# Loading the down weights of the experts from ScalarE's queue in place of SyncE's, in a two-block transformer on one core

## What is computed

```python
def expert_block(args):
    xe, e = args
    return (jax.nn.silu(xe @ w_gate[e]) * (xe @ w_up[e])) @ w_down[e]
```

## Time and profile before

| | us |
|---|---|
| median of 3 executions | 2813.23 |
| lowest and highest of them | 2811.11, 2819.49 |
| the profiled execution's own time | 2816.55 |
| its span (first to last instruction) | 2814.5 |
| PE busy | 2575.6 (92%) |
| DVE busy | 1076.7 (38%) |
| ACT busy | 749.4 (27%) |
| POOL busy | 237.4 (8%) |
| DMA moved | 623.91 MB, mean 222 GB/s |

### The profile page before, as it was taken

One profiled execution on the slowest core, in us unless ns is written; L12 is line 12 of the kernel. 1 busy time (PEld: TensorE's weight loads), 2 busy tenths in 40 slices (PEclk: granted clock), 3 DMA queues, 4 the chain that ended last, 5 costly groups with the idle time before them and its releaser, 6 DMA issues. The chain is left out here.

```text
span 2814.5 us, 51444 instructions
## 1 busy us (share of the span) xinstructions
PE 2575.6 (92%) x20439; PEld 1525.9 (54%) x20439; DVE 1076.7 (38%) x2661; ACT 749.4 (27%) x1601; POOL 237.4 (8%) x405
## 2 busy tenths in 40 slices
PE   7999999999999999999997878789999899888787
PEld 4544655544654467645655555544576466555554
DVE  2582653582653245557221111153443642111114
ACT  1211531211642157521111111143675111111111
POOL 4000011000010000011010001020000111110011
PEclk9999999999999999999999999999999999999999
DMA  9211842222843100236999999973002499999996
GB/s 337 90 60 68 299 144 94 88 75 75 299 128 128 60 1 2 84 149 224 396 389 399 394 405 402 399 280 112 1 2 91 176 346 399 397 403 411 414 403 241
DMA packets 134846, 623.91 MB, mean 222 GB/s; under 512 B 14480, under 2 KB 18672, under 8 KB 106496
## 3 DMA queue, kind: packets, MB, share of 16 engines
q1 hardware_dynamic: 103424, 519.68, 47.6%
q0 software_dynamic: 31232, 101.57, 10.5%
HBM read 573.59 MB, written 47.61 MB: 221 GB/s over the span
## 5 line engine op out<-in xcount | busy, mean ns | idle before, releaser
L1236 PE MATMUL PJ<-WR,XT 128*128 128x512 f32 (+2 forms) x1152 | 475.3, 568 | 5.7 <-ACT XT L182 2.8
L182 ACT ACTIVATE PT<-TR 128x512 f32<-128x512 f32 (+3 forms) x384 | 172.9, 480 | 962.2 <-PE TR L1468 832.7
L1236 PEld LDWEIGHTS PJ<-WR,XT 128*128 128x128 f32 x1152 | 215.6, 191 | 243.9 <-issue 215.7
L182 DVE TENSOR_TENSOR PR<-G 128x256 f32<-128x256 f32 (+1 forms) x64 | 29.6, 463 | 686.6 <-ACT G L182 686.2
L1445 PE MATMUL SC<-QK,XT 128*64 128x256 f32 x2112 | 244.3, 385 | 39.1 <-DMA QK<-in_w_up_dram 25.4
L1445 PE MATMUL SC<-WR,XT 128*64 128x256 f32 x1984 | 228.6, 383 | 43.1 <-DMA WR<-in_w_up_dram 25.3
L1194 PE MATMUL PJ<-WR,XT 128*128 128x512 f32 x576 | 254.4, 597 | 3.4 <-ACT XT L182 2.5
L182 DVE TENSOR_REDUCE SM<-SC 128x1 f32<-128x768 f32 (+6 forms) x208 | 173.7, 835 | 172.1 <-PE SC L1214 167.2
L1396 PE MATMUL PJ<-WR,XT 128*128 128x512 f32 x512 | 227.4, 596 | 1.0 <-issue 1.0
L1445 PEld LDWEIGHTS SC<-QK,XT 128*64 128x64 f32 x2112 | 154.6, 138 | 123.6 <-DMA QK<-in_w_up_dram 35.4
L1445 PEld LDWEIGHTS SC<-WR,XT 128*64 128x64 f32 x1984 | 141.5, 138 | 126.9 <-DMA WR<-in_w_up_dram 35.3
(11 more groups left out here) (277 smaller groups left out, 2766.7 us busy)
## 6 DMA issues: line engine op xcount, KB each, us to landing
QK<-in_w_gate_dram SPq DMA_DIRECT2D x34, 2048.0 KB, 23.7
WR<-in_w_down_dram SPq DMA_DIRECT2D x34, 2048.0 KB, 20.2
QK<-in_w_up_dram SPq DMA_DIRECT2D x32, 2048.0 KB
WR<-in_w_up_dram SPq DMA_DIRECT2D x32, 2048.0 KB
WR<-in_w_gate_dram SPq DMA_DIRECT2D x30, 2048.0 KB, 23.4
QK<-in_w_down_dram SPq DMA_DIRECT2D x30, 2048.0 KB
WR<-in_w_ada_dram SPq DMA_DIRECT2D x24, 2048.0 KB, 8.8
WR<-in_w_in_dram SPq DMA_DIRECT2D x14, 2048.0 KB, 7.8
```

The lines of the kernel that those rows point to most:

```text
L182: return lambda *a, **k: Signal(make(*a, **k), self)
L1236: m = mm(bank[:, 0:n], XT1[:, c, s.t * P:(s.t + 1) * P], w[:, c, 0:n], start=c == 0, stop=c == DC - 1)
```

## The change

`load_expert` moves out of SP's function and gets the issuing engine as an argument. SP loads d0 and d1 as before, and from then on only gate and up weights. ACT waits once for the table `ORD`, and loads d2 before its step of place 1; at the end of each of its steps r it waits until `down(r)` is done, reads the expert's number of place r+2 from `ORD`, and issues d(r+2) on its own queue. Its last loads are d30 and d31; its step 30 is written out without a load. Buffers, semaphores, shapes and the order on PE stay.

```diff
--- before.py
+++ after.py
@@ -1053,6 +1053,19 @@
             for r in range(evenly.stop, end):
                 go(lambda a, b: b, r)
 
+        def load_expert(eng, u, e, near_rows=False):
+            tile = slot_tile(u.slot)
+            name = {"gate": "w_gate_2", "up": "w_up_2", "down": "w_down_2"}[u.kind]
+            src = ins[name][u.l, bass.ds(e, 1), :, :].rearrange("e k n -> (e k) n")
+            if u.kind == "down" and near_rows:
+                eng.dma_start(tile.rearrange("p (h x) -> p h x", h=2), src.rearrange("(h p c) n -> p h (c n)", h=2, c=2)).then_inc(
+                    w_loaded[u.slot], 16)
+            elif u.kind == "down":
+                eng.dma_start(tile.rearrange("p (c n) -> p c n", c=4), src.rearrange("(c p) n -> p c n", p=P)).then_inc(
+                    w_loaded[u.slot], 16)
+            else:
+                eng.dma_start(tile, src.rearrange("(p c) n -> p (c n)", p=P)).then_inc(w_loaded[u.slot], 16)
+
         block = ctx.enter_context(nc.Block())
 
         def w_ready(eng, u):
@@ -1088,19 +1101,6 @@
                     sp.dma_start(tile, w_dram[u.kind](u).rearrange("(c p) n -> p c n", p=P)).then_inc(
                         w_loaded[u.slot], 16)
 
-            def load_expert(u, e, near_rows=False):
-                tile = slot_tile(u.slot)
-                name = {"gate": "w_gate_2", "up": "w_up_2", "down": "w_down_2"}[u.kind]
-                src = ins[name][u.l, bass.ds(e, 1), :, :].rearrange("e k n -> (e k) n")
-                if u.kind == "down" and near_rows:
-                    sp.dma_start(tile.rearrange("p (h x) -> p h x", h=2), src.rearrange("(h p c) n -> p h (c n)", h=2, c=2)).then_inc(
-                        w_loaded[u.slot], 16)
-                elif u.kind == "down":
-                    sp.dma_start(tile.rearrange("p (c n) -> p c n", c=4), src.rearrange("(c p) n -> p c n", p=P)).then_inc(
-                        w_loaded[u.slot], 16)
-                else:
-                    sp.dma_start(tile, src.rearrange("(p c) n -> p (c n)", p=P)).then_inc(w_loaded[u.slot], 16)
-
             attended = {u.l: u.pj + 1 for u in (s.u for s in steps if s.kind == "weigh") if u.kind in ("window", "global", "ctx")}
             n = 0
             while n < len(units):
@@ -1115,16 +1115,15 @@
                 sp.wait_ge(pj_full, attended[l])
                 for k in range(8):
                     free(m[k].prev)
-                    load_expert(m[k], m[k].e)
+                    load_expert(sp, m[k], m[k].e)
                 sp.wait_ge(order_ready, l + 1)
 
                 def two_experts(i, r):
                     expert = {p: sp.value_load(ORD[0:1, bass.ds(i * 2 + (r + p - 2), 1)], min_val=0, max_val=EXPERTS - 1)
-                              for p in (2, 3, 4)}
-                    for k in range(8, 14):
-                        down = m[k].kind == "down"
-                        sp.wait_ge(pj_full if down else sc_full, i * (4 if down else 2) + (m[k - 6].done + (r - 2) * (2 if down else 1)))
-                        load_expert(m[k], expert[m[k].e], small(m[k].e + r - 2))
+                              for p in (3, 4)}
+                    for k in (k for k in range(8, 14) if m[k].kind != "down"):
+                        sp.wait_ge(sc_full, i * 2 + (m[k - 6].done + r - 2))
+                        load_expert(sp, m[k], expert[m[k].e], small(m[k].e + r - 2))
 
                 mixed = LARGE - 1
                 with sp.Fori(0, (mixed - 2) // 2) as i:
@@ -1132,9 +1131,9 @@
                 two_experts(0, mixed)
                 with sp.Fori(0, (EXPERTS - 4 - mixed) // 2) as i:
                     two_experts(i, mixed + 2)
-                for k in range(92, 96):
+                for k in (k for k in range(92, 96) if m[k].kind != "down"):
                     free(m[k].prev)
-                    load_expert(m[k], m[k].e)
+                    load_expert(sp, m[k], m[k].e)
                 n += 3 * EXPERTS
                 if l < DEPTH - 1:
                     for u in units[n:n + 3]:
@@ -1832,12 +1831,25 @@
                     x_in(once, 2)
                     hidden(once, 1)
 
+                    down_unit = {u.e: u for u in units if u.kind == "down" and u.l == s.l}
+
+                    def load_down(at_, r):
+                        act.wait_ge(pj_full, at_(4, J0 + 2 * (r - 2) + 2))
+                        e = act.value_load(ORD[0:1, bass.ds(at_(2, r), 1)], min_val=0, max_val=EXPERTS - 1)
+                        load_expert(act, down_unit[r], e, small(r))
+
                     def step(at_, r):
                         hidden_turned(at_, r)
                         x_in(at_, r + 2)
                         hidden(at_, r + 1)
-
-                    places(act, 1, EXPERTS - 1, step)
+                        load_down(at_, r + 2)
+
+                    act.wait_ge(order_ready, s.l + 1)
+                    load_down(once, 2)
+                    places(act, 1, EXPERTS - 2, step)
+                    hidden_turned(once, EXPERTS - 2)
+                    x_in(once, EXPERTS)
+                    hidden(once, EXPERTS - 1)
                     hidden_turned(once, EXPERTS - 1)
                     for g in range(2):
                         use = s.tr[g - 2]
```

## The result

The changed kernel takes **2832.96 us** (median of 5 runs, 2827.61 to 2836.74), the kernel before 2813.09 us beside it (5 runs, 2811.11 to 2819.49): a ratio of **1.0061, 95% interval 1.0046 to 1.0076**. The change costs 0.6%, 17 us by the ratio and 19.9 by the two medians. The forecast was 2819 with a range from 2803 to 2839: right that nothing is won, short by 14 us.

The account below looks back on a forecast made before the run. The prediction took full DMA engines to bound the small places and PE the large ones. Two layers at 3 us each, 0 elsewhere, added 6 us to the median 2813.2, giving 2819, range 2803 to 2839.

Parts of the forecast that it names:

- no wait of SP held up a load: SP's load order: its waits follow PE's own order, so no buffer is refilled earlier; 0 us.
- none of ACT's work came late: ACT, each place: wait, table read and DMA issue are covered by at least 7.4 us before its copy; cost 0.
- POOL's slack: POOL's queue: a gather lands after 6.6 us and is first used 19.2 us after issue; cost 0.
- the bound that I had set: Places: the prediction is wrong if a pair becomes shorter or longer by over 0.4 us.
- turns by record: DMA engines, between queues: about one record of each queue in turn, not equal bytes; the forecast itself, +6 us, chance 0.40.
- The end of each layer is where the order costs: Last loads of each layer: part of d30 passes before u31, 3 us a layer, 2 x 3 = +6 us.
- taken in turn they finish together, the same place time: Small places: 16 records of 16 KB and 16 of 8 KB on each engine, 14.9 us plus POOL's share; unchanged place time.
- No stall: Small and large places: a down lands some 17 us after issue, needed about 28.7 us later in small places; no wait.
- Three queues lose bandwidth: Small places: the loss near POOL's transfers may double, 23 us, with the 6 us 2842; chance 0.12.
- Downs overtake entirely: Last two loads of each layer: up to 10.2 us move in front of u31, 2834; chance 0.15, block-wise turns included.
- nothing moves: Whole kernel: both queues drained as issued, or a shift under 1 us, 2813; chance 0.20.
- a gain: Small places: two queues move bytes faster, 23 us less and 6 more, 2796, half of it 2808; chance 0.13.

Follow-up runs that it names:

- the first kernel of the experiments: The changed kernel with SP again loading the downs of places 29, 30 and 31, ACT those of 2 to 28: 2825.14 us against 2816.17 (1.0041).
- the switch in the middle: Two kernels against the one before: ACT loads downs to place 18, then SP, 2824.39 us (1.0027); ACT loads only those of 19 to 28, 2823.40 us (1.0011).

## Why the prediction was right or wrong

**Right: no wait of SP held up a load, so nothing was won, and none of ACT's work came late.** The share of the DMA engines is 1.01, and ACT's idle time before the copy of the turned product is 256.3 us in 18 places, 14.2 us each, for 14.0 before. POOL's slack covered the gather: it lands 4 us later and PE waits for none. PE's waits for steady downs are gone and those for up weights have grown, as forecast. A steady place is neither shorter nor much longer: from place 15 to 29 of layer 1 a pair takes 32.6 us for 32.2, in layer 0 it is 0.1 us more. The 0.4 us are at the bound that I had set, and 1.1% less rate would make about as much.

**Right: turns by record.** The reading of the earlier trace rows holds between two queues of weights as well: 189 of 189 successors of SP's records are ACT's, and with 4 KB records it is the downs that come late. The same page of the Trainium skill, section "Rules for kernel authors", holds that DMAs spread over SP, ACT and GpSimd gain no bandwidth and save only issue time; the trace agrees that none is gained (114.92 MB for 116.22), and adds that the spreading isn't free.

**Wrong: "The end of each layer is where the order costs", 3 us a layer.** The step compared what stands in front of u31 alone, and there it found half of d30. It took for granted that all up to place 29 stays, because "taken in turn they finish together, the same place time". The place time is nearly the same, but the places are shifted: once the first small places have passed, one block more (0.7 of a down, 0.3 of a gate) has passed in front of every up block. I had all that was needed. The forecast has a down land some 17 us after its issue, and the up weights issued shortly before it 27.36 us after theirs; comparing those two would have shown a whole down of 5.2 us in front. (The 17 us were too short as well: downs land after 20.3 and 22.2 us, the medians in 2440 to 2740.) In place of 3 us a layer, 7.7 were measured at place 15, and 9.6 at u31.

**Wrong: that the end pays only for u31.** PE itself needs 15.7 us from u30 to u31 at the least (the first kernel of the experiments, with each group at 3.6 us), so of a lag that u30 has only 2.3 us can be made good by a u31 that is early. I had set 8 us at u31 as the point at which I would be wrong, and it is 9.6 in both layers.

**"No stall" was wrong at one place.** In the passage from large to small places PE waits 2.18 us for down(8) (layer 0: 2.22, 2.89 and 0.86 us for three downs), issued at 2394.08 and landed after 24.01 us in the chain of waits. The share of the DMA engines stays at 1.01 through it, with 383 GB/s for 393 in 2390 to 2420 us, 0.7 us worth of bytes.

**The rival "Three queues lose bandwidth"** is true to a small part. It gave 23 us; the trace shows 1.1 and 0.5% of bytes less, 4 and 2 us, and the switch in the middle about 2 us a layer. With POOL's gathers cut, the loss of rate is gone and the cost of the change falls from 20 to 11.7 us. "Downs overtake entirely" named 10.2 us a layer in front of u31: the number is close to the 9.6 measured, but its reason, more than a record for a record, is not what happened. The other two rivals, nothing moves and a gain, fell. That 2833 lies in the range of 2803 to 2839 is thus in part luck: the sum gave 2819, and the upper end came from these two rivals, of which one has another reason and the other is true only to a small part. One reading in the prediction is off without moving the sum: of a small place's bytes a third, not half, come in 8 KB records.

No kernel here that does all the work beats the kernel before; the nearest, ACT from place 19 to 28, is slower by 0.11% with an interval that begins at 0.01%. What PE's lower granted clock costs in the small places (0.91 for 0.97) was not measured by itself. PE waits for weights there at either, but SP's next issue waits for the group that has become longer, and in both layers u30's group takes 5.1 to 5.4 us for 3.7, 1.4 to 1.7 of the 9.6 us at u31.

## What to carry to other kernels

When the DMA engines are full, moving a load to another queue doesn't add bandwidth but changes the order in which bytes arrive, and a load that now lands before it is needed was paid for by one that is needed first. Compare, for the load on the critical path, what has passed in front of it in the old order and in the new, at the first places as well as at the last: issue time plus landing time of each shows it. The larger part of the cost is a stock, paid once where the queues part, so it shows neither in the time of a steady place nor in the DMA share; plot the start of each place against the kernel before to see it.

## What the runs showed that was not expected

The granted clock in the small places, a mean over times at 2.4 GHz (1.00) and at 1.2 GHz, fell from 0.97 and 0.95 to 0.91 and 0.90 though PE did no more work. PE waits for loads no longer than before (50 us for 58 in 2440 to 2740), but in one piece a place, and after the longer of these pieces a group of 32 matmuls takes 5.1 to 6.5 us instead of 3.7 (2759.26 above; over the group at 2496.36 the granted clock is 0.71, over a group of 3.7 us at 2562.72 it is 1.00). POOL's gather, which moves little, lands 4 us later once a second queue of weights runs beside it, though the bytes in all are no more, and its stores of rows landed after 8.3 us for 6.0.
